# One single-core encoder step: attention products as single float32 matmuls in place of three split ones

## What is computed

```python
h = rms_norm(x) @ w_in                                   # q, k, v of mixers A, B, C, D
# A: stick-breaking     w = exp(log_sigmoid(z) + later), z = q @ k.T / 8, keys strictly before the query
# B: window of 128 keys plus own chunk, 4 query heads on 2 kv heads, sinks and a bias
# C: differential       w = softmax(q1 @ k1.T / 32**.5 + bias) - lam * softmax(q2 @ k2.T / 32**.5 + bias)
# D: own chunk and 8 before it, relative bias
o = w @ v                                                # per head, 64 columns; C: RMSNorm of its rows
x = x + concat(A, B, C, D) @ w_out
```

## Time and profile before

| | us |
|---|---|
| median of 3 runs | 1783.87 |
| all runs | 1776.14, 1783.87, 1784.74 |
| profiled execution: its own time | 1776.1 |
| its span, first to last instruction | 1776.3 |
| PE busy | 1693.1 (95%), 9,689 matmuls |
| PE weight loads busy | 1511.5 (85%) |
| DVE / ACT / POOL busy | 826.3 / 456.9 / 259.8 |
| mean granted TensorE clock | 0.888 of 2.4 GHz |

### The profile page before, as it was taken

The page is one execution under the profiler, slowest core; times in us unless marked ns, Lnnn a source line. Parts: engine busy times, 40 slices in busy tenths (PEclk is TensorE's granted clock), DMA queues, the critical chain, the costliest instruction groups (busy, mean ns, idle before and its releaser), DMA issues.

```text
span 1776.3 us, 25708 instructions
## 1 busy us (share of the span) xinstructions
PE 1693.1 (95%) x9689; PEld 1511.5 (85%) x9689; DVE 826.3 (47%) x1617; ACT 456.9 (26%) x1160; POOL 259.8 (15%) x437
## 2 busy tenths in 40 slices
PE   5999999799987999999799999999999999999997
PEld 4999999687865777778687899999999999999996
DVE  6111111678665555667722542442543524425425
ACT  4211112545564433455612101001000010010002
POOL 7000000245245322331022100000000000000001
PEclk9999999679575555659899999999999999999999
DMA  7111110400000000010120410111111101111002
GB/s 226 37 47 35 47 47 15 151 1 2 1 1 1 1 0 1 1 72 2 67 82 1 142 48 25 47 47 47 47 44 50 47 24 47 47 47 47 0 0 112
DMA packets 90737, 75.88 MB, mean 43 GB/s; under 512 B 5928, under 2 KB 83273, under 8 KB 90653
## 3 DMA queue, kind: packets, MB, share of 16 engines
q1 hardware_dynamic: 90668, 75.01, 13.7%
HBM read 64.06 MB, written 10.77 MB: 42 GB/s over the span
## 4 chain that ended last, share of the span: by engine, by line
PE 89%; DVE 4%; POOL 3%; ACT 1%; issue 1%; DMA 1%; SPq 1%; ACTq 0%; POOLq 0%; DVEq 0%
PE acc L677 28%; PE acc L678 26%; PE acc L679 26%; PE acc L813 5%; PE acc L846 1%; POOL xlo L1460 1%; PE acc L855 1%; PE acc L759 1%; PE acc L927 1%; PE acc L692 1%; DVE hT_r L1335 1%; DVE hT_r L1311 0%; DVE hT L1248 0%; DVE hT L1258 0%; DMA hT<-in_x_prompt_dram 0%
## 5 line engine op out<-in xcount | busy, mean ns | idle before, releaser
L677 PE MATMUL acc<-ohi,gu_hi 128*128 128x384 f32 (+1 forms) x1056 | 344.3, 326 | 2.8 <-DVE gu_lo L1159 1.9
L679 PE MATMUL acc<-ohi,gu_lo 128*128 128x384 f32 (+1 forms) x1056 | 344.2, 326 | 0.0
L678 PE MATMUL acc<-olo,gu_hi 128*128 128x384 f32 (+1 forms) x1056 | 344.0, 326 | 0.0
L677 PEld LDWEIGHTS acc<-ohi,gu_hi 128*128 128x128 f32 x1056 | 198.2, 188 | 3.8 <-issue 3.3
L678 PEld LDWEIGHTS acc<-olo,gu_hi 128*128 128x128 f32 x1056 | 198.2, 188 | 0.4
L679 PEld LDWEIGHTS acc<-ohi,gu_lo 128*128 128x128 f32 x1056 | 198.2, 188 | 0.0
L1107 ACT ACTIVATE silu<-acc 128x384 f32<-128x384 f32 (+1 forms) x66 | 31.3, 474 | 639.7 <-PE acc L679 638.6
L1384 DVE TENSOR_TENSOR prod<-acc,silu 128x384 f32<-128x384 f32 (+1 forms) x66 | 35.3, 535 | 336.7 <-ACT silu L1107 336.7
L677 PE MATMUL acc<-xhi,win_hi 128*128 128x384 f32 (+1 forms) x528 | 173.1, 328 | 0.0
L679 PE MATMUL acc<-xhi,win_lo 128*128 128x384 f32 (+1 forms) x528 | 172.5, 327 | 0.0
L678 PE MATMUL acc<-xlo,win_hi 128*128 128x384 f32 (+1 forms) x528 | 172.5, 327 | 0.0
(11 more groups left out here) (179 smaller groups left out, 3121.4 us busy)
## 6 DMA issues: line engine op xcount, KB each, us to landing
win_raw<-in_w_in_dram SPq DMA_DIRECT2D x22, 512.0 KB, 3.9
ffn_raw<-in_w_gate_dram SPq DMA_DIRECT2D x22, 512.0 KB, 3.8
ffn_raw<-in_w_up_dram SPq DMA_DIRECT2D x22, 512.0 KB, 4.4
ffn_raw<-in_w_down_dram SPq DMA_DIRECT2D x22, 512.0 KB, 4.1
hT<-in_x_prompt_dram SPq DMA_DIRECT2D x8, 512.0 KB, 7.0
hT<-in_w_out_dram SPq DMA_DIRECT2D x8, 512.0 KB, 5.0
x<-in_x_prompt_dram SPq DMA_DIRECT2D x8, 512.0 KB, 5.9
out_dram<-y_out SPq DMA_DIRECT2D x8, 512.0 KB, 2.6
```

The costliest lines, as they stand in the source:

```text
L677: pe.matmul(out, a_hi, b_hi, start=first, stop=False)
L678: pe.matmul(out, a_hi, b_lo, start=False, stop=False)
L679: return pe.matmul(out, a_lo, b_hi, start=False, stop=last)
```

## The change

Attention's products are made from the values themselves, in plain float32. The scores are one float32 matmul for each piece of keys, with q as the weight as before. For the products with V the operands change places: the turned probabilities (up to 128 keys by 128 queries) are loaded as the weight and the 64 columns of V stream by, so the output comes out as 128 queries by 64 and needs no second turn. Gone are all splits of q, k, V and of the probabilities, `turn_value`, `oT_one` and ACT's copy to it, and the semaphores around them. ACT alone copies the turned probabilities (`probs_t`), and `batch_copied` becomes `pt_copied` (ACT) and `o_copied` (DVE). Some waits that the splits had carried move: PE's first B job waits for the swapped keys, its first sample unit of A for the cached V, and ACT waits for the stores of V's rows before it writes the output's parts over them. The input projection, the output projection and SwiGLU keep their three products.

```diff
-                for c, k, k_low in keys(job):
-                    mm = split_product(acc[0:job.rows, base + c:base + c + k.shape[1]], high, low, k, k_low,
-                                       True, True)
+                for c, k in keys(job):
+                    mm = pe.matmul(acc[0:job.rows, base + c:base + c + k.shape[1]], hT[p, job.q_tile, cols], k,
+                                   start=True, stop=True)
                 mm.then_inc(scores_ready, 1)
...
-                    mm = split_product(bank(6 + u % 2, job.rows, 64), high, low, pt_hi[u % 2][0:w, t, 0:job.rows],
-                                       pt_lo[u % 2][0:w, t, 0:job.rows], t == 0, t == job.blocks - 1)
+                        rows = v_rows[0:w, job.first + t, v]
+                    mm = pe.matmul(bank(6 + u % 2, 64, job.rows), probs_t[u % 2][0:w, t, 0:job.rows], rows,
+                                   start=t == 0, stop=t == job.blocks - 1)
                 mm.then_inc(pv_done, 1)
-
-            def turn_value(u):
-
-                n = units[u][0].rows
-                pe.wait_ge(oT_copied, u + 1)
-                pe.transpose(bank(6 + u % 2, 64, n, 256), oT_one[:, u % 2, 0:n], ident[0:64, 0:64])\
-                    .then_inc(oT_turned, 1)
...
-                u = unit_at(r - NORM_LAG)
-                if u is not None:
-                    n = units[u][0].rows
-                    act.wait_ge(pv_done, u + 1)
-                    if u >= 2:
-                        act.wait_ge(oT_turned, u - 1)
-                    act.copy(oT_one[:, u % 2, 0:n], bank(6 + u % 2, n, 64)).then_inc(oT_copied, 1)
...
-                            ins = act.copy(pt_hi[u % 2][to], src)
-                        ins.then_inc(pt_hi_ready, 1)
+                            ins = act.copy(probs_t[u % 2][to], src)
+                        ins.then_inc(pt_copied, 1)
...
-                        for src, to in batch_parts(u, b):
-                            ins = dve.tensor_tensor(pt_lo[u % 2][to], src, pt_hi[u % 2][to].bitcast(F32), ALU.subtract)
-                        ins.then_inc(batch_copied, 1)
```

More of the change, by code:

```diff
@@ L133, in build @@
     p_index = {n: i for i, n in enumerate(p_batches)}
+    o_batches = [n for key, n in sorted(batches.items(), key=lambda kv: kv[1]) if key[0] == "o"]
+    o_index = {n: i for i, n in enumerate(o_batches)}
     with ExitStack() as ctx:
@@ L480, in build @@
         CHUNK_SPLITS = [12, 18, 24]
[L484 to L508, removed]
         def wait_weights(eng, u):
@@ L791, in scores @@
                     pe.wait_ge(exp_done, job.n - 1)
[L792 to L795, removed]
+                if job.n == first_job["B"]:
+                    pe.wait_ge(swap_in, 64)
                 base = 2 * (job.n % 2) * 512
                 p, cols = slice(job.p0, job.p0 + job.dim), slice(job.q_col, job.q_col + job.rows)
-                high, low = q_hi[p, job.head // 2, cols], hT_r[p, job.q_tile, cols]
-                for c, k, k_low in keys(job):
-                    mm = split_product(acc[0:job.rows, base + c:base + c + k.shape[1]], high, low, k, k_low,
-                                       True, True)
+                for c, k in keys(job):
+                    mm = pe.matmul(acc[0:job.rows, base + c:base + c + k.shape[1]], hT[p, job.q_tile, cols], k,
+                                   start=True, stop=True)
                 mm.then_inc(scores_ready, 1)
@@ L830, in values @@
                     if t % 4 == 0:
[L831 to L835, removed]
[L836 to L839 removed]
+                        pe.wait_ge(pt_copied, p_index[batches[("p", u, t // 4)]] + 1)
+                    if job.i == SAMPLE and t < job.past:
+                        rows = v_cache[0:w, job.first + t, v]
+                    elif job.i == SAMPLE:
+                        rows = v_rows[0:w, NT - 1, v]
+                    else:
+                        rows = v_rows[0:w, job.first + t, v]
+                    mm = pe.matmul(bank(6 + u % 2, 64, job.rows), probs_t[u % 2][0:w, t, 0:job.rows], rows,
+                                   start=t == 0, stop=t == job.blocks - 1)
                 mm.then_inc(pv_done, 1)
[L842 to L847 removed]
             def turn_out(u):
@@ L1020, in probabilities @@
                                    accum_out=row_sum[0:n, job.n:job.n + 1]).then_inc(exp_done, 1)
-            def high_qk(m, at, to):
-                if at == 0:
-                    if m != "A":
-                        act.wait_ge(scores_ready, first_job[m])
-                    if m == "B":
-                        act.wait_ge(swap_in, 64)
-                for src, high, _ in qk_parts(m)[at:to]:
-                    act.copy(high, src).then_inc(qk_hi_ready, 1)
-            def high_v(m, at, to):
-                if at == 0:
-                    if m != "A":
-                        act.wait_ge(pv_done, first_unit[m])
-                    act.wait_ge(vrow_out[m], 16 * sum(kv_target(m, j) is not None for j in range(NT)))
-                    act.wait_ge(vcache_in, 16 * N_CACHE)
-                for src, high, _ in v_parts(m)[at:to]:
-                    act.copy(high, src).then_inc(v_hi_ready, 1)
             act.wait_ge(prep_dve, n_eng["dve"])
@@ L1081, in _ @@
             act.wait_ge(pv_done, NU)
-            act.wait_ge(batch_copied, len(batches))
+            act.wait_ge(o_copied, len(o_batches))
+            for m in "ABCD":
+                act.wait_ge(vrow_out[m], 16 * sum(kv_target(m, j) is not None for j in range(NT)))
             for kind, e, c in OUT_SPLITS:
@@ L1305, in _ @@
                     scan(jobs[r - 1])
-                u = unit_at(r - T_LAG)
-                if u is not None:
-                    for b in range(-(-units[u][0].blocks // 4)):
-                        dve.wait_ge(pt_hi_ready, p_index[batches[("p", u, b)]] + 1)
-                        for src, to in batch_parts(u, b):
-                            ins = dve.tensor_tensor(pt_lo[u % 2][to], src, pt_hi[u % 2][to].bitcast(F32), ALU.subtract)
-                        ins.then_inc(batch_copied, 1)
                 u = block_at(r - OT_LAG)
@@ L1510, in output_root @@
                     .then_inc(c_factor, 1)
-            def low_half(kind, m, part):
-                parts, per_mixer, ready, done = ((qk_parts(m), QK_PARTS, qk_hi_ready, qk_split) if kind == "qk"
-                                                 else (v_parts(m), V_PARTS, v_hi_ready, v_split))
-                src, high, low = parts[part]
-                count = per_mixer * "ABCD".index(m) + part
-                pool.wait_ge(done, count)
-                pool.wait_ge(ready, count + 1)
-                pool.tensor_tensor(low, src, high.bitcast(F32), ALU.subtract).then_inc(done, 1)
-            next_round = 0
-            for u, unit in enumerate(units):
-                while next_round <= unit[-1].n + 1:
-                    for kind, m, at, to in splits_at(next_round):
-                        if on_pool(m, at):
-                            low_half(kind, m, at)
-                    next_round += 1
+            for u, unit in enumerate(units):
                 a, b, n = unit[0], unit[-1], unit[0].rows
```

103 lines of the change are left out of this document (26 added, 77 removed).

## The result

The changed kernel takes 1935.46 us (median of 4 runs, 1922.31 to 1938.18), the kernel before 1784.13 (4 runs): 1.086 times as long, 95% interval 1.081 to 1.092. The forecast was 1930 with a range of 1795 to 1965. The profiled execution is 160 us longer than that of before (spans 1936.4 and 1776.3). Run again beside the experiments, the kernel before took 1771 to 1805 us at mean granted clocks of 0.889 to 0.867, so a ratio to it is sure to about 1%, and one variant is better compared with another.

What follows compares the result with a forecast made beforehand. PE bounds the attention stage except at mixer starts. At 1.2 GHz, streams 610, seams 32 and 29, starts 15 make 686 us against 536.7: +150 on 1776.1, 1926, given as 1930; range 1795 to 1965, its own 1880 to 1965.

Steps and rivals of the forecast that it cites:

- The clock: Attention stage: PE at 1.2 GHz from the start of A to the end of D, 2.4 afterwards.
- The rows behind that reason: Trace of C before: clock rose twice behind dense V products (2.4 of 3.4 us, 2.7 of 3.5), once lost without them.
- A V pass: New V products: loading 128 columns and streaming 64 takes 0.213 us a pass, 0.426 a block, against 0.33 before.
- rival 3: V products: loads hide, a pass costs 107 ns at 1.2 GHz, 100 us less, 1830 us; chance 0.08.
- A float32 product: Scores: two instructions, four cycles a column against three; 3.33 ns a key column at 1.2 GHz in place of 2.5.
- Seams: PE passing between kinds of work: 0.3 us for 108 units of A, B, D (32), 0.8 for 36 of C (29).
- Starts: Where mixers begin: 10 us off in C's first units, about 3 at each other start; 15 us of waiting left.
- the 16 us given as a sign: Start of C: its first 8 jobs in about 16 us would show the forecast right.
- By mixer: Stage +150 us over before: A +69, B +10, C +22, D +49.
- The last addition: Whole kernel: 1926 us for the profiled execution, median of runs 7.7 us above it, given as 1930.
- Rival 1: Attention stage: the clock keeps its earlier pattern, mean 0.65; +22 us, some 1800 us; chance 0.15.
- Rival 2: Attention stage: without turns and pauses PE is dense enough for 2.4 GHz throughout; 386 us, about 1630 in all; chance 0.10.

Runs made afterwards that it cites:

- the padded kernel: Changed kernel with scores over all 128 rows (q copied by ACT into zero-padded tiles), V products still 64 columns a pass: 1641.65 us, ratio to before 0.918.
- the wide kernel: Changed kernel with 128 columns of V (the head's and its neighbour's) streaming past each loaded block of probabilities, half of them read: 1739.31 us, ratio to before 0.974.
- the padded split one: Kernel before, with high and low parts of q in zero-padded tiles so scores use all 128 rows; products stay three split ones: 1720.41 us, 0.962.
- the opposite kernel: Changed kernel with zero-padded q in mixers A, B and D alone, C scoring with 32 rows: 1737.18 us, ratio to before 0.976.

## Why the prediction was right

The course of the clock and the size were right, and the reason given for the clock was one half of it. That 1930 lies within 6 us of 1935 is in part luck, as the mixers below show. By its steps:

- **The clock.** 1.2 GHz from the start of A to the end of D, 2.4 after, as forecast. The reason given (V passes stream for half of their time and wait for the load in the other) is shown as far as the V products go: they alone take the clock away (1897 us), and filling them brings it back (1739). It is not enough, though. The sentence "the scores use 64 rows or 32 as before" stood there as a side remark; the padded kernel shows it is the other half: with 128 rows the half-filled V passes do no harm. Where both are thin, the clock was 0.50 throughout; where the scores alone are thin it came and went (0.50 for 164 us of C in the wide kernel); with full scores it was 0.92 to 1.00 in every mixer of the padded changed kernel, whose V is thin, and 0.82 to 0.90 in the padded split one, whose V is full and where PE waits more.
- **The rows behind that reason** were two among several. In the same trace 2.24 of 3.4 us of V products (691.0 to 694.4 us) were followed by 0.50, and 1.52 of 3.4 us (796.8 to 800.2) by 0.99. The rows alone could not show what the clock follows; the experiments did. The two stretches, instructions that touch `v_hi` alone, as there:

```profile
691.00:694.40 3.40, 2.24 (x14) 2.21 (x14) 0.00 (x0) 0.00 (x0) 0.00 (x0) 0.50 0.00 0
796.80:800.20 3.40, 1.52 (x8) 1.40 (x8) 0.00 (x0) 0.00 (x0) 0.00 (x0) 0.50 0.00 0
```

- **A V pass** was put at 0.213 us between a bound of 0.107 and the load not overlapped. Its median from start to start is 0.213 at 1.2 GHz (sixteen passes in 3.44 us) and 0.112 in the padded kernel at 2.4. That ends rival 3. The row could not decide it: if the load took 0.107, a stream of 0.107 behind it would also make 0.21. The wide kernel does: there a stream of 0.213 hides the load wholly, so behind a stream of 0.107 the load itself must take the 0.213. The estimate from the Trainium skill (TensorE: Matmul & The Clock Gate, LDWEIGHTS) of 107 ns for 128 columns fits at 2.4 GHz and not at 1.2: the load follows the clock.
- **A float32 product**: 0.85 us a record at 512 columns, two records, as forecast.
- **Seams** were put at 0.3 us a unit of A, B and D. The unit of D above shows 0.30 ahead of the scores, 0.05 at the transpositions and 0.03 at V: 0.38. Over 108 units that would be 9 of the 11 us by which the stage was forecast too short (686, measured 697). The 0.3 had no row at 1.2 GHz; the earlier trace rows less the turn give 0.36.
- **Starts.** C's first eight jobs, from PE's first scores to those of the ninth job, take 13.8 us against 25.1: 11 less, 10 forecast. The 26.3 us of the earlier trace rows begin 5 us into C and are not those eight jobs, so the 16 us given as a sign were too many, and the 10 us taken off were right. For other engines PE waited 8.5 us in the whole stage, against 15 in the sum.
- **By mixer**: forecast +69, +10, +22 and +49 on the earlier trace rows. Measured +62.5, +14, +27 and +57 (176.9, 88.4, 270.8, 160.8 against 114.4, 74.3, 244.0, 104.0); the borders of the earlier trace rows lie up to 2 us from PE's first scores. A came out 6.5 us shorter than forecast, B, C and D 4, 5 and 8 longer, and these errors partly cancel. A is shorter in spite of its longer seams, so the seams are not the whole account; the rest I did not follow up.
- **The last addition** was 4 us off: 1926 and 7.7 make 1934, not 1930.
- **Rival 1** (the clock keeps its pattern) did not occur in the change. A pattern like that of before came in the two runs with V as the weight, which take 1828 and 1834 us; their work is not that of the change, so its price of 1800 stays untested.
- **Rival 2** (the clock stays up, about 1630) did not occur by itself, but its price was near: the padded kernel, with a granted clock of 0.94 in the stage and ACT's copies on top, takes 1642. The condition I gave for it, PE dense enough, was wrong as I meant it. PE is busy 50.00 of 50 us at 0.50 in the changed kernel and 146 of 177 at 0.92 in the padded one. The Trainium skill (TensorE: Matmul & The Clock Gate, Part 1) says that activity releases the throttle; read as busy time, these two windows contradict it.

## What to carry to other kernels

Before fewer instructions are traded for other shapes, look at what fraction of the array streams in each: a pass that loads 128 columns and streams 64, or scores over 32 or 64 rows, can leave TensorE at 1.2 GHz however busy it looks. If the clock line shows half under a fully busy PE, fill the array with zero rows or unneeded columns that ride behind a load anyway; here that gave 294 and 196 us. Judge a change of shapes with the clock restored on both sides as well: here the change is 8.6% slower as made, and with both sides padded its form is the faster one.

## What the runs showed that was not expected

- Rows with zeros in the weight raise the clock here: no column and no product was added on PE, and C went from a granted clock of 0.50 to 0.92.
- Columns that nobody reads cost nothing beside a 128-column load: 0.213 us a pass at 1.2 GHz with 128 columns and with 64, 0.112 at 2.4 GHz with either. Both load and stream cover all 128 rows, so here the load of the next weight runs beside the stream of the last over the same rows.
- The clock is regained and lost in the middle of a stage, but not at once. In the kernel padded in C alone it rose 33 us after C's first scores, behind short jobs in which PE also waits, and in C of the opposite kernel it fell 2 us after C's first scores.
